# Attention steps of up to 512 score columns made of segments, placement at multiples of 64 bytes, and the low parts of weights by two GpSimd instructions

## The reference

```
s = q k^T * scale + mask ;  m = max(s) ;  p = exp(s - m)
out = (p / sum(p) * gate) v
```

## Time and profile before

| | |
|---|---|
| time, median of 3 runs | 2784.76 us (2782.76 to 2787.28) |
| the profiled execution's own time | 2784.23 us |
| its span | 2782.3 us |
| mean granted clock of PE | 0.995 of full speed |
| chain that ended last | PE 89%, DVE 6%, ACT 3%, issue 1% |
| L604, L605, L606 in that chain | 25% of the span each |

### The profile page before, as it was taken

One profiled execution on the slowest core, in us unless ns is written; L12 is line 12 of the kernel. 1 busy time (PEld: TensorE's weight loads), 2 busy tenths in 40 slices (PEclk: granted clock), 3 DMA queues, 4 the chain that ended last, 5 costly groups with the idle time before them and its releaser, 6 DMA issues.

```text
span 2782.3 us, 37597 instructions
## 1 busy us (share of the span) xinstructions
PE 2719.6 (98%) x13426; PEld 2221.6 (80%) x13426; DVE 1028.7 (37%) x1931; ACT 1099.7 (40%) x1791; POOL 1272.4 (46%) x713
## 2 busy tenths in 40 slices
PE   8999999999999999999999999999999999999997
PEld 7857888888867888888868888888887788888886
DVE  6664322114453322105545334222047652422202
ACT  7565332225564332223255334232237443423321
POOL 4644444444444444444544634444444473444442
PEclk9999999999999999999999999999999999999999
DMA  4301222333201223232313412222322341232231
GB/s 179 114 2 39 98 90 98 99 105 102 98 31 57 98 90 105 99 106 72 113 47 99 144 46 76 98 98 98 106 77 98 106 151 46 66 110 97 94 108 63
DMA packets 69222, 252.08 MB, mean 91 GB/s; under 512 B 7680, under 2 KB 7936, under 8 KB 68864
## 3 DMA queue, kind: packets, MB, share of 16 engines
q1 hardware_dynamic: 68112, 247.43, 26.5%
q10 hardware_dynamic: 1008, 3.28, 0.4%
HBM read 248.58 MB, written 2.10 MB: 90 GB/s over the span
## 4 chain that ended last, share of the span: by engine, by line
PE 89%; DVE 6%; ACT 3%; issue 1%; POOL 0%; DMA 0%; DVEq 0%; SPq 0%; POOLq 0%; ACTq 0%
PE ps L604 25%; PE ps L606 25%; PE ps L605 25%; PE ps L771 3%; PE ps L806 3%; PE ps L792 2%; PE ps L713 1%; PE ps L715 1%; PE ps L714 1%; DVE ps L1983 1%; DVE x L1987 1%; DVE xl L1638 1%; DVE pr L1730 1%; PE ps L1013 1%; PE ps L1014 1%
## 5 line engine op out<-in xcount | busy, mean ns | idle before, releaser
L519 POOL TENSOR_TENSOR w_lo<-w_raw,w_hi 128x1024 fp32r<-128x1024 f32 x460 | 1109.4, 2416 | 1293.1 <-ACT w_hi L1133 1290.2
L604 PE MATMUL ps<-xh,w_hi 128*128 128x512 f32 x2260 | 884.5, 391 | 13.3 <-POOL w_lo L519 6.8
L606 PE MATMUL ps<-xh,w_lo 128*128 128x512 f32 x2260 | 879.6, 389 | 0.0
L605 PE MATMUL ps<-xl,w_hi 128*128 128x512 f32 x2260 | 879.5, 389 | 0.0
L1133 ACT ACTIVATE w_hi<-w_raw 128x1024 fp32r<-128x1024 f32 x462 | 485.1, 1055 | 532.2 <-PE ps L606 474.9
L604 PEld LDWEIGHTS ps<-xh,w_hi 128*128 128x128 f32 x2260 | 424.3, 188 | 108.6 <-issue 14.1
L606 PEld LDWEIGHTS ps<-xh,w_lo 128*128 128x128 f32 x2260 | 424.2, 188 | 88.6
L605 PEld LDWEIGHTS ps<-xl,w_hi 128*128 128x128 f32 x2260 | 424.4, 188 | 87.9 <-issue 1.0
L606 PE MATMUL ps<-hh,w_lo 128*128 128x512 f32 x704 | 273.9, 389 | 0.0
L604 PE MATMUL ps<-hh,w_hi 128*128 128x512 f32 x704 | 273.9, 389 | 0.0
L605 PE MATMUL ps<-hl,w_hi 128*128 128x512 f32 x704 | 273.9, 389 | 0.0
(11 more groups left out here) (299 smaller groups left out, 3011.2 us busy)
## 6 DMA issues: line engine op xcount, KB each, us to landing
w_raw<-weights_in SPq DMA_DIRECT2D x462, 512.0 KB, 3.2
x<-x_in SPq DMA_DIRECT2D x4, 512.0 KB, 7.4
mem<-mem_in ACTq DMA_DIRECT2D x2, 1024.0 KB, 4.8
x_out<-x SPq DMA_DIRECT2D x4, 512.0 KB, 2.6
rope<-rope_in SPq DMA_DIRECT2D x1, 512.0 KB, 10.2
tab<-tables_in ACTq DMA_DIRECT2D x2, 256.0 KB, 2.7
tab<-tables_in SPq DMA_DIRECT2D x1, 384.0 KB, 10.6
small<-small_in ACTq DMA_DIRECT2D x1, 326.5 KB, 4.9
```

The costliest lines, as they stand in the source:

```text
L519: nc.gpsimd.tensor_tensor(w_lo[:, slot], w_raw[:, slot], w_hi.bitcast(f32)[:, slot], ALU.subtract).then_inc(lo_ready, 1)
L604: nc.tensor.matmul(dst, w_hi[:, slot, w], hi, start=first, stop=False)
L605: nc.tensor.matmul(dst, w_hi[:, slot, w], lo, start=False, stop=False)
L606: return nc.tensor.matmul(dst, w_lo[:, slot, w], hi, start=False, stop=last)
```

## The change

Three things change.

1. A step is now a list of segments (`seg`), each with its own group, two units and a first column `at`. Two segments share one step if their columns add up to 512 or less. `steps_layer0` and `steps_causal` write the order out: tile 3 alone, tile 2 with tile 0, tile 1 with itself. In U0 the B branch has steps of its own. Scores, minima, exponentials, normalising and values run per segment; transposes, copies to `pt`, the reciprocal and the semaphores run per step. `den`, `negm` and `wgt` have a further axis for the segment. The iterations of the compressed branch's hooks and the order of its tiles are new.
2. A tensor of 32 bytes, `up_to_64_bytes`, stands behind the small ones.
3. `low` issues two instructions of 512 columns instead of one of 1024; the second signals.

```diff
-        den = sb("den", [P, 4, 2])
-        negm = sb("negm", [P, 4, 2])
-        wgt = sb("wgt", [P, 4, 2])
+        den = sb("den", [P, 4, 2, 2])
+        negm = sb("negm", [P, 4, 2, 2])
+        wgt = sb("wgt", [P, 4, 2, 2])
         c4 = sb("c4", [P, 8])
         c8 = sb("c8", [P, 8])
         lp = sb("lp", [P, 4, 8])
         negsink = sb("negsink", [P, 8])
+        sb("up_to_64_bytes", [P, 8])
...
+        def seg(group, two, opens=True, closes=True):
+            return dict(group=group, two=two, opens=opens, closes=closes, begins=False, ends=False, at=0)
+
+        def step(*segs):
+
+            at = 0
+            for sg in segs:
+                sg["at"] = at
+                at += sg["two"][0]["nk"]
+            return list(segs)
+
+        def width(st):
+            return st[-1]["at"] + st[-1]["two"][0]["nk"]
...
+            m0, m1, m2, m3 = (main(t) for t in range(TB))
+            b0, b1, b2, b3 = (other(t) for t in range(TB))
+            steps = [step(sg) for sg in m3]
+            steps += [step(m2[0]), step(m2[1])] + [step(m2[i + 2], m0[i]) for i in range(6)] + [step(m0[6], m0[7])]
+            for j in range(4):
+                steps += [step(b0[j]), step(m1[2 * j], m1[2 * j + 1])]
+            for j in range(4):
+                steps += [step(b1[j]), step(b2[j])]
+            return with_banks(steps + [step(sg) for sg in b3], (4, 5))
...
+                g0, g1, g2, g3 = (group(t, half) for t in range(TB))
+                for i in range(4):
+                    steps += [step(g3[i]), step(g2[i], g0[i])]
+                steps += [step(g1[0], g1[1]), step(g1[2], g1[3])]
...
-        CMP_ORDER = (3, 0, 2, 1)
-        CMP_SCORES, CMP_MASKED, CMP_EXP = (1, 3, 14, 26), (1, 3, 15, 27), (1, 4, 16, 28)
-        CMP_WEIGHTS, CMP_TURNED, CMP_COPY = (1, 4, 17, 29), (2, 5, 18, 30), (2, 6, 19, 31)
+        CMP_ORDER = (3, 2, 0, 1)
+        CMP_SCORES, CMP_MASKED, CMP_EXP = (1, 4, 8, 14), (1, 4, 9, 15), (1, 5, 10, 16)
+        CMP_WEIGHTS, CMP_TURNED, CMP_COPY = (1, 6, 11, 17), (2, 7, 12, 18), (2, 8, 13, 19)
...
             def low(slot):
-                nc.gpsimd.tensor_tensor(w_lo[:, slot], w_raw[:, slot], w_hi.bitcast(f32)[:, slot],
+                w = w_hi.bitcast(f32)
+                half = CT * P // 2
+                nc.gpsimd.tensor_tensor(w_lo[:, slot, 0:half], w_raw[:, slot, 0:half], w[:, slot, 0:half],
+                                        ALU.subtract)
+                nc.gpsimd.tensor_tensor(w_lo[:, slot, half:], w_raw[:, slot, half:], w[:, slot, half:],
                                         ALU.subtract).then_inc(lo_ready, 1)
...
+                    for a in range(2):
+                        for i, sg in enumerate(st):
+                            u = sg["two"][a]
+                            p = pr[:, (2 * n + a) % 8, sg["at"]:sg["at"] + u["nk"]]
+                            w = wgt[:, n % 4, i, a:a + 1]
+                            gate = ones[:, 0:1] if u["gate"] is None else u["gate"]
+                            last = nc.gpsimd.tensor_scalar(p, p, w, gate, ALU.mult, ALU.mult)
+                        last.then_inc(pn_ready, 1)
...
-                two = [(u, 2 * (s0 + s) + a) for a, u in enumerate(steps[s]["two"])]
-                for u, n in two:
+                n0 = 2 * (s0 + s)
+                for n in (n0, n0 + 1):
                     if n >= 3:
                         pe.wait_ge(sm_done, n - 2)
-
-                parts = len(two[0][0]["qk"])
-                for c in range(parts):
-                    for u, n in two:
-                        q, k = u["qk"][c]
-                        last = nc.tensor.matmul(ps[:, S_BANKS[n % 3], 0:u["nk"]], q, k,
-                                                start=c == 0, stop=c == parts - 1)
-                        if c == parts - 1:
-                            last.then_inc(s_ready, 1)
+                for sg in steps[s]:
+                    parts, cols = len(sg["two"][0]["qk"]), slice(sg["at"], sg["at"] + sg["two"][0]["nk"])
+                    for c in range(parts):
+                        for a, u in enumerate(sg["two"]):
+                            q, k = u["qk"][c]
+                            last = nc.tensor.matmul(ps[:, S_BANKS[(n0 + a) % 3], cols], q, k,
+                                                    start=c == 0, stop=c == parts - 1)
+                            if sg is steps[s][-1] and c == parts - 1:
+                                last.then_inc(s_ready, 1)
...
+                        for sg in steps[s - LAG]:
+                            g = sg["group"]
+                            if sg["begins"] and mts.n + g["after"]:
+                                pe.wait_ge(mixl_ready, mts.n + g["after"])
+                            for places in side_by_side(sg["two"]):
+                                blocks = len(places[0][3])
+                                for kb in range(blocks):
+                                    for a, rows, column, values in places:
+                                        last = nc.tensor.matmul(
+                                            ps[rows, g["bank"], tokens(column)], values[kb],
+                                            pt[:, (n + a) % 4, tokens(sg["at"] // P + kb)],
+                                            start=sg["opens"] and kb == 0,
+                                            stop=sg["closes"] and kb == blocks - 1)
+                            if not sg["closes"] and not sg["opens"]:
+                                last = last_of(sg)
...
-                A(p, p, ACT.Exp, scale=-1.0, bias=negm[:, slot, a:a + 1],
-                  accum_out=den[:, slot, a:a + 1]).then_inc(p_ready, 1)
+                for i, sg in enumerate(steps[s]):
+                    u = sg["two"][a]
+                    p = pr[:, n % 8, sg["at"]:sg["at"] + u["nk"] + (u["sink"] is not None)]
+                    last = A(p, p, ACT.Exp, scale=-1.0, bias=negm[:, slot, i, a:a + 1],
+                             accum_out=den[:, slot, i, a:a + 1])
+                last.then_inc(p_ready, 1)
...
+                    for a in range(2 if s < len(steps) else 0):
...
+                        for i, sg in enumerate(steps[s]):
+                            u = sg["two"][a]
+                            cols, start = slice(sg["at"], sg["at"] + u["nk"]), 3.0e38
+                            if u["sink"] is not None:
+                                start = negsink[:, u["sink"]:u["sink"] + 1]
+                                V.tensor_copy(pr[:, n % 8, u["nk"]:u["nk"] + 1], start)
+                            if i == 0:
+                                dve.wait_ge(s_ready, n + 1)
+
+                            last = V.tensor_tensor_reduce(out=pr[:, n % 8, cols], in0=ps[:, S_BANKS[n % 3], cols],
+                                                          in1=u["mask"], scale=-u["scale"], scalar=start, op0=ALU.add,
+                                                          op1=ALU.min, accum_out=negm[:, slot, i, a:a + 1])
+                        last.then_inc(sm_done, 1)
...
+                        before, n_segs = (slot - 1) % 4, len(steps[s - 1])
+                        V.reciprocal(wgt[:, before, 0:n_segs], den[:, before, 0:n_segs]).then_inc(wgt_ready, 1)
```

More of the change, by code:

```diff
@@ L359, in tokens, with with_banks @@
             return slice(t * P, (t + 1) * P)
[L361 to L372, removed]
+        def with_banks(steps, banks):
+            segs = [sg for st in steps for sg in st]
+            names = [sg["group"]["name"] for sg in segs]
             free = [(0, b) for b in banks]
             n = 0
[L375 to L379, removed]
+            for s, sg in enumerate(segs):
+                sg["begins"] = names[s] not in names[:s]
+                sg["ends"] = names[s] not in names[s + 1:]
+                if sg["begins"]:
+                    sg["group"]["after"], sg["group"]["bank"] = free.pop(0)
+                if sg["ends"]:
+                    sg["group"]["number"] = n
                     n += 1
-                    free.append((n, st["group"]["bank"]))
+                    free.append((n, sg["group"]["bank"]))
             return steps
@@ L430, in group @@
                         two.append(unit(qk, (t + 1) * P, tab[:, T - (t + 1) * P:T], scale, [(rows, i, vals)]))
[L431 to L435, removed]
+                    segs.append(seg(g, two))
+                return segs
+            steps = []
+            for half in range(halves):
+                g0, g1, g2, g3 = (group(t, half) for t in range(TB))
+                for i in range(4):
+                    steps += [step(g3[i]), step(g2[i], g0[i])]
+                steps += [step(g1[0], g1[1]), step(g1[2], g1[3])]
+            return with_banks(steps, banks)
         def steps_memory(banks):
@@ L446, in group @@
                     two.append(unit(qk, MEM, tab[:, 0:MEM], 1 / 16, places))
-                return [step(new_group(t, half), two)]
-            return in_turns([(group(t, 0), group(t, 1)) for t in range(TB)], banks)
```

(10 more changed lines are left out.)

69 lines of the change are left out of this document (17 added, 52 removed).

## The result

The changed kernel takes 2793.34 us (median; 2791.83 to 2798.56, 12 runs) against 2782.78 us for the kernel before, measured on the same chip (2780.51 to 2788.76, 12 runs). The ratio is 1.0036, 95% interval 1.0028 to 1.0044: **slower by 10 us**, where 2761 and "faster" were predicted. The time is also outside the range of 2748 to 2778.

A forecast was written before the change was run, and what follows sets the result against it. PE's order was taken to bound the attention stages, through its fixed cost a step. Steps 14.5 plus waits 10 minus halves 1 make 23.5 us off 2784.2: 2760.7, as a median 2761; range 2748 to 2778.

The forecast's parts named there:

- The alignment: Tensors behind the enlarged small ones move by 128 bytes, staying at multiples of 64 if there before: 0 us.
- the slower one: Rival, 6%: in merged attention steps PE waits for DVE to free score banks, 0.95 us a step, giving 2798 us.
- nothing moved in the linear layers: Sign to watch if the forecast holds: the linear layers, which the change doesn't touch, stay as they were.
- Fixed part of 29 steps: Attention stages: 29 fewer steps at 0.55 us fixed PE cost, less 1.5 for segments: 14.5 us saved (bounds 3.8, 16.0).
- Waits, 10: Attention stages: of 24.2 us of PE waiting, 14 stay and 10 are saved (bounds 0 and 18).
- near 103, 63 and 34: Predicted us for the attention stages of layer 0 (U0), layer 1 (U1) and forget attention (UF), from 114.1, 72.0, 39.6.
- A merged step keeps 0.05 us a segment: Attention: a merged step's second segment, its own score and value matmul group, costs PE 0.05 us, 1.5 in all.
- The one foreseen at s = 8 of U0: Layer 0 attention: PE's compressed scores wait for ACT's copy at the end of the same step, 1.3 us.
- The rival that the waits move along: Rival, 22%: the attention steps' fixed part goes, but each wait returns in fewer, fuller steps: 2771 us.
- The halves: Low parts in two POOL instructions: +0.20 us each, about 92 us of POOL, 1 us lost (bounds 4 gained, 4 lost).
- the rival that the halves free DVE: Rival, 12%: at the start, 5 of PE's 6.8 us of waits for lows go instead of 1 being lost: 2755.
- the rival priced at 7%: Rival, 7%: in attention, segments keep their fixed cost and the waits stay, saving 3.8 - 1: 2781 us.

The follow-up runs named there:

- e3: The kernel before with an unused 128-byte tensor ahead of its small tensors and everything allocated behind them, nothing else changed: 2812.31 us, ratio 1.0102.
- e10: The changed kernel with a filler tensor of 160 bytes instead of 32, the same kernel as e4 run again: 2764.73 us, ratio 0.9936.
- e11: The kernel of e10 with each low part in one GpSimd instruction instead of two halves: 2764.72 us, ratio 0.9937.
- e9: A small separate program of 48-matmul blocks, weights or activations shifted by various bytes, no other engine computing: 227 ns a matmul at shift 0, 512 columns.
- e6: The kernel before with only the two weight tensors moved by 128 bytes, all else in place: 2834.84 us, ratio 1.0177.
- e7: As e3, the kernel before with an unused tensor there, but of 64 bytes instead of 128: 2836.93 us, ratio 1.019.
- e5: The kernel before with 128 unused bytes ahead of the weights, so everything PE reads moves together: 2783.63 us, ratio 0.9995.
- e4: The changed kernel with a filler tensor of 160 bytes instead of 32: 2763.62 us, ratio 0.9926.

## Why the prediction was wrong, step by step

- **The alignment, 0 us: this step failed.** The prediction said that what stands behind the new bytes "moves by two times 64 bytes, so if it was at a multiple of 64 it still is: 0". That the tensors move by 128 bytes was right. The fault was to take a multiple of 64 as what matters and so to price the move at nothing, with no bound on the side of a loss. The shift by itself costs 28.0 us in e3 (2812.31 - 2784.36), and undoing it gives back 28.6 in e10 (2793.34 - 2764.73). No rival covered it; the slower one was about score banks, and PE's waits for them fell in all three stages (6.1, 4.6 and 5.0 us to 3.4, 1.8 and 3.1). The list of what to watch had the right item, "nothing moved in the linear layers", and it is the item that broke. The Trainium skill (page "SBUF — State Buffer", section "Operand start alignment") asks only that an operand start at a multiple of its element size and says that this is about legality, not speed. The shifts of 4 to 224 bytes are all legal by it, and at 512 columns they cost 2 to 7 ns a matmul.
- **Fixed part of 29 steps, 14.5 us: right. Waits, 10: the size was off, within the bounds.** Together 24.5; the run after shows 21.7. e10 shows 24.6, and that it meets the 24.5 is luck, as its clock will show. Its stages:

```profile
128.91:233.54 104.63, 95.82 (x930) 67.92 (x929) 73.92 (x326) 70.03 (x236) 53.39 (x94) 1.00 0.01 2
775.88:838.42 62.54, 59.55 (x594) 43.78 (x593) 41.95 (x157) 46.03 (x140) 35.20 (x60) 1.00 0.01 2
1396.83:1430.74 33.91, 30.00 (x313) 23.34 (x312) 21.73 (x73) 22.72 (x66) 16.73 (x28) 1.00 0.01 2
```

  Predicted were "near 103, 63 and 34". The granted clock over U0 is 1.00 here, 0.97 in the run after and 0.97 in the run before. In the run after PE idles 1.4 us on `s_c` at s = 12, and in the next 3 us the granted clock lies near the 1.2 GHz level, as in the earlier trace rows; at the end of U0 it does so again (0.53 from 234 to 237):

```profile
168.00:171.00 3.00, 3.00 (x15) 2.45 (x16) 2.43 (x13) 2.85 (x10) 1.81 (x4) 0.59 0.00 0
```

  e10 has the same wait and keeps its clock there. 0.03 x 107.5 = 3.2 us is about the difference between the two U0 stages (2.9). So the saving in U0 has to be taken between stages with the same clock. At 0.97 it is 114.1 - 107.5 = 6.6. At 1.00 there is e3, the kernel before with its shift:

```profile
131.54:242.54 111.00, 102.04 (x930) 66.62 (x929) 76.87 (x347) 72.49 (x247) 53.32 (x94) 1.00 0.01 2
```

  111.0 - 104.6 = 6.4. The like-for-like saving of all three stages is therefore near 21.7, not 24.6. The steps alone, 29 x 0.55 with segments that cost nothing (next point), are 6.0 + 6.6 + 3.3 = 16.0 us (11, 12 and 6 steps). What is left for the waits is 0.5 + 2.8 + 2.4 = 5.7 where 10 was forecast. This split rests on the formula; no run separates the two.
- **A merged step keeps 0.05 us a segment: a little less.** The timeline of PE in U1 of the run after (start and length in us):

```profile
794.29 1.14 PE L798 MATMUL ps<-k_r,q_r 64*128 64x384 f32 x8
795.36 1.09 PE L819 MATMUL ps<-ident,pr 128*128 128x128 f32 x8
796.38 1.09 PE L834 MATMUL ps<-pt,v_t 128*64 128x128 f32 x16
797.40 1.13 PE L798 MATMUL ps<-k_r,q_r 64*128 64x512 f32 x4
...
800.51 0.91 PE L798 MATMUL ps<-k_r,q_r 64*128 64x384 f32 x4
```

  The merged step takes 797.40 - 794.29 = 3.11 us and the one with a single segment 800.51 - 797.40 = 3.11: in this pair two segments cost nothing over one. The formula from the earlier trace rows gave 3.07.
- **The waits that remain.** The one foreseen at s = 8 of U0 is there, 0.9 us on ACT's `pc_t` where 1.3 was said, and the one at s = 12 (1.4 on `s_c`) was foreseen one step early. In U1 and UF waits for minima are 1.8 and 3.1 us, against 4.6 and 5.0. The rival that the waits move along fell there: all waits that the profile names for PE go from 5.3 to 2.8 and from 5.6 to 3.9 us. In U0 it held: the sum is 8.6 us before and after. Minima fall from 6.1 to 3.4, but waits for DVE's copies of the transposes rise from 1.0 to 2.9 and those of the compressed branch from 1.5 to 2.3.
- **The halves, 1 us lost: size off, within the bounds.** A half is 1292 ns in the median where 1298 was taken from the earlier trace rows, so +0.19 a chunk, and POOL is busy 1345 us, not 1272 (73 more, where 92 were estimated). None of it reaches PE: e10 and e11 are level. PE's waits for lows before the attention are 6.8 us with whole lows and 4.2 with halves in the run after; from 1456 us on they are 1.6 and 4.0. So the rival that the halves free DVE got 2.6 of the 5 us that it assumed, and 2.4 came back later.

With the alignment term put right, the prediction's sum is 2784.2 - 24.5 + 1 + 28 = 2789, and the profiled run took 2794.94. Of the 6 us left, 2.8 are in the attention stages (21.7 saved instead of 24.5: the waits) and 3.5 elsewhere (32.5 lost instead of 29). The second is no larger than the scatter between runs of one kernel (2 to 8 us here). That e10 gains 24 us by its profiled run (2760.0) but 17 by its median is such scatter, and a part of it may go with the clock: among e10's five runs the fastest, that one, has a mean granted clock of 0.996 and the slowest (2767.27) 0.993.

Two sums of the prediction don't come out as written. Its bounds added straight give 2746 to 2774, not 2748 to 2772, and the rival priced at 7% enters its last sum with 0.06. Neither changes the verdict.

## What to carry to other kernels

An edit that grows a small tensor moves all tensors allocated behind it; compute the addresses of the matmuls' streamed operand and weights before and after, and treat a change of their difference modulo 256 bytes as a cost of its own, here 1 to 2% of the kernel. Its size is to be measured: neither the forecast for 64 bytes nor the map of a small program gave it. When PE is 98% busy, busy share and waits can't show such a loss: count matmuls in a fixed stretch, or compare the mean length of one, in a stage that the edit doesn't touch. A change of several parts can hold a gain and a larger loss: the segments were worth 17 to 21 us and were hidden by 32 bytes of filler that should have been 160. And a stage's time is compared between runs with the same granted clock in that stage; here stages that differ in the clock differ by 3 us of 105.

## What the runs showed of the hardware

- With PE working alone (e9), the pace of matmuls of 512 columns on fp32r tensors, the type of the high and low parts, depends on where the streamed operand starts against the weights, modulo 256 bytes: 227 ns at 0, 229 at 192 (weights ahead), 232 to 234 at the other multiples of 32. Everything moved by 128 together has 227.5. In the full kernel a move by 128 bytes costs 28 us with `xl` left in place (e3) and 49 with all products apart (e6), and one by 64 costs 52 with `xl` left in place (e7). Moving everything together costs nothing (e5).
- At 256 columns the difference is turned round and smaller: 120.0 ns at 0, 117.3 to 119.8 elsewhere, one block each.
- One operand out of place slows the matmuls next to it too: with only the low activations moved by 128 bytes, all three kinds of a block slow down, while in the changed kernel, where the low activations are the ones in place, their matmuls keep their 389 ns. With the high ones moved by 64 bytes (e7) the unmoved low ones take 397.
- A step whose scores and values come in two groups, of 384 and 128 columns, costs PE what one with a single group of 512 does (3.11 us each, in the pair shown).
- With half the granted clock for 3.4 us the same stage was 1.4 us longer (U0 of e4, 106.0 us with one such fall; U0 of e10, 104.6 without).
